# Row norms as a product with a diagonal matrix, in a two-block transformer kernel on one core

## The reference

```python
def rms_norm(x, g):
    xf = x.astype(jnp.float32)
    y = xf * lax.rsqrt(jnp.mean(xf * xf, axis=-1, keepdims=True) + EPS)
    return (y * g.astype(jnp.float32)).astype(x.dtype)

# first block, per layer: feed-forward, attention (forgetting or dilated), feed-forward
h = modulate(rms_norm(x, norm_g[i, 0]), shift[:, 0], scale[:, 0])
x = x + MACARON_WEIGHT * gate[:, 0, None, :] * swiglu(h, ...)

# second block, per layer: a mixer, then a convolutional feed-forward
h = rms_norm_2(x, norm_mix_pre[l]);  y = mixer(h);               x = x + rms_norm_2(y, norm_mix_post[l])
h = rms_norm_2(x, norm_ffn_pre[l]);  y = conv_ffn(h, ...);       x = x + rms_norm_2(y, norm_ffn_post[l])
```

## Time and profile before

| | |
|---|---|
| three timed runs | 1896.79, 1892.59, 1892.78 us; median 1892.78 |
| profiled execution | 1897.27 us, its span 1895.5 us, mean granted clock 0.98 |
| TensorE busy | 1805.1 us, 95% of the span |
| VectorE busy | 1463.1 us, 77% |
| ScalarE busy | 1053.0 us, 56% |
| chain that ended last | PE 75%, DVE 13%, issue 6%, ACT 4% |

### The profile page before, as it was taken

How to read it: one execution, slowest core, us unless ns; L and a number is a source line. 1 busy time by engine, 2 the same in 40 slices (tenths; PEclk the granted TensorE clock), 3 DMA queues, 4 the chain that set the end, 5 groups by cost and what they waited for, 6 DMA issues and landing times.

```text
span 1895.5 us, 28442 instructions
## 1 busy us (share of the span) xinstructions
PE 1805.1 (95%) x9778; PEld 1510.0 (80%) x9778; DVE 1463.1 (77%) x2268; ACT 1053.0 (56%) x1602; POOL 131.7 (7%) x170
## 2 busy tenths in 40 slices
PE   5999899899999999999999999999889998989998
PEld 4888677788878888788878888878678887768886
DVE  6888787688888887867755566557779966868994
ACT  5554465655445543655454455544776646666663
POOL 1101011000110110000000000000012200002210
PEclk9999999999999999999999999999999999889999
DMA  9878666377888786554530355554255454224553
GB/s 384 337 274 311 236 241 209 136 250 280 280 291 295 281 283 224 186 180 176 187 122 1 127 204 183 193 205 154 75 181 196 180 189 153 103 89 173 183 193 117
DMA packets 63778, 382.03 MB, mean 202 GB/s; under 512 B 7154, under 2 KB 7410, under 8 KB 27587
## 3 DMA queue, kind: packets, MB, share of 16 engines
q1 hardware_dynamic: 42912, 300.96, 44.3%
q0 software_dynamic: 20208, 78.79, 11.6%
q10 hardware_dynamic: 578, 1.22, 0.2%
HBM read 379.90 MB, written 1.05 MB: 201 GB/s over the span
## 4 chain that ended last, share of the span: by engine, by line
PE 75%; DVE 13%; issue 6%; ACT 4%; DMA 1%; DVEq 1%; SPq 0%; ACTq 0%
PE ps L560 18%; PE ps L477 11%; PE ps L479 10%; PE ps L478 10%; PE ps L562 9%; DVE ring_lo L1615 3%; DVE wb L1914 2%; PE ps L608 1%; PE ps L581 1%; PE ps L583 1%; PE ps L582 1%; PE ps L836 1%; PE ps L862 1%; DVE wa L1903 1%; PE ps L849 1%
## 5 line engine op out<-in xcount | busy, mean ns | idle before, releaser
L1615 DVE TENSOR_TENSOR ring_lo<-ring,w_hi 128x1024 fp32r<-128x1024 f32 x534 | 666.5, 1265 | 256.0 <-ACT w_hi L1130 254.5
L1130 ACT ACTIVATE w_hi<-ring 128x1024 fp32r<-128x1024 f32 x556 | 579.2, 1057 | 451.7 <-PE ps L479 269.3
L560 PE MATMUL ps<-h_both,w_hi 128*128 128x512 f32 x1984 | 700.8, 398 | 0.0
L562 PE MATMUL ps<-h_both,ring_lo 128*128 128x256 f32 x1984 | 557.6, 281 | 0.0
L560 PEld LDWEIGHTS ps<-h_both,w_hi 128*128 128x128 f32 x1984 | 373.4, 188 | 91.0
L562 PEld LDWEIGHTS ps<-h_both,ring_lo 128*128 128x128 f32 x1984 | 375.7, 189 | 0.0
L477 PE MATMUL ps<-w_hi,h_both 128*128 128x512 f32 x580 | 236.2, 407 | 7.6 <-DVE h_both L2348 3.4
L479 PE MATMUL ps<-w_hi,h_both 128*128 128x512 f32 x580 | 229.4, 395 | 0.0
L478 PE MATMUL ps<-ring_lo,h_both 128*128 128x512 f32 x580 | 228.9, 395 | 0.0
L477 PE MATMUL ps<-w_hi,hid_lo 128*128 128x512 f32 x456 | 180.3, 395 | 1.2 <-DVE ring_lo L1615 1.1
L479 PE MATMUL ps<-w_hi,hid_hi 128*128 128x512 f32 x456 | 177.6, 389 | 0.0
(11 more groups left out here) (360 smaller groups left out, 2150.9 us busy)
## 6 DMA issues: line engine op xcount, KB each, us to landing
ring<-in_stream SPq DMA_DIRECT2D x276, 1024.0 KB, 4.8
arena<-in_mod POOLq DMA_DIRECT2D x128, 512.0 KB, 5.7
arena<-in_mod SPq DMA_DIRECT2D x14, 512.0 KB, 13.9
gate<-in_wide POOLq DMA_DIRECT2D x3, 1536.0 KB, 10.0
arena<-in_nsaw POOLq DMA_DIRECT2D x2, 1072.0 KB, 9.0
ring<-in_stream SPq DMA_DIRECT2D x4, 512.0 KB, 15.1
arena<-in_konst POOLq DMA_DIRECT2D x1, 1295.5 KB, 8.7
arena<-in_mixw POOLq DMA_DIRECT2D x2, 576.0 KB, 10.5
```

The lines of the kernel that those rows point to most:

```text
L560: nc.tensor.matmul(ps[:, banks[b], :].rearrange("p (w t) -> p w t", w=2), hi, h_both[:, :, 2 * r + i, :], start=(r == 0 and i == 0), stop= ...
L562: mm = nc.tensor.matmul(ps[:, banks[b], T:2 * T], lo, h_hi[:, 2 * r + i, :], start=False, stop=(r == 3 and i == 1))
L1130: nc.scalar.activation(w_hi[:, q % SPLITS, :], ring[:, half % SLOTS, (q % 2) * QUARTER:(q % 2 + 1) * QUARTER], ACT.Copy).then_inc(w_hi_rea ...
L1615: v.tensor_tensor(ring_lo[:, slot, cs], ring[:, slot, cs], w_hi[:, q % SPLITS, :], ALU.subtract).then_inc(w_lo_ready, 1)
```

## The change

Norms 1 to 9 no longer form the scaled rows. A 128x128 diagonal matrix with the reciprocal roots of a tile's 128 tokens is formed (`rdiag`, 2 x 128 columns at the start of `xn`), and TensorE multiplies: chunk of x, stationary, by the diagonal. The result is the transposed and scaled chunk, as before. Norm 0 keeps its transposes.

- Tile 0's diagonal is formed by ScalarE (identity times the reciprocal), between the two halves of tile 1's squares. VectorE's reciprocal for it stands inside the update of x, between its last product and its last addition (`first_tile`).
- Tile 1's diagonal is formed by VectorE in `norm`, one instruction of 128 columns.
- In `update_normed` the first half of tile 1 is multiplied by the gate before the reciprocal is known (behind a new semaphore, `yms_half`), then scaled and added to x in one instruction.

```diff
+        rdiag = xn[:, 0, 0:2 * P]
...
@@ TensorE
-                        mm = turn(c, tt)
+            def norm(m):
+                for tt in range(NT):
+                    pe.wait_ge(xn_ready, 4 + 2 * (m - 1) + tt + 1)
+                    for c in range(KC):
+                        if c == 4 and tt == 0:
+                            pe.wait_ge(x_ready, 2 * m)
+                        b, o = norm_at(m, c)
+                        mm = nc.tensor.matmul(ps[:, b, o + tt * P:o + (tt + 1) * P], x[:, tt, c * P:(c + 1) * P], rdiag[:, tt * P:(tt + 1) * P], start=True, stop=True)
...
@@ ScalarE, norm
                 tick.mark(nc.scalar.activation(ms[:, 4:5], ms[:, 1:2], ACT.Identity, bias=eps_col))
+                act.wait_ge(rstd_ready, NT + m)
+                nc.scalar.activation(rdiag[:, 0:P], ident, ACT.Copy, scale=rstd[:, 0:1]).then_inc(xn_ready, 1)
                 act.wait_ge(x_ready, 2 * m)
...
@@ ScalarE, post_norm
-                tick.mark(nc.scalar.activation(ms[:, 6:7], ms[:, 3:4], ACT.Identity, bias=eps_col))
+                nc.scalar.activation(ms[:, 6:7], ms[:, 3:4], ACT.Identity, bias=eps_col).then_inc(yms_half, 1)
...
@@ VectorE
+            def first_tile(m):
+                dve.wait_ge(ms_ready, 2 * m + 1)
+                v.reciprocal(rstd[:, 0:1], rms[:, 0:1]).then_inc(rstd_ready, 1)
             def norm(m):
-                for tt in range(NT):
-                    dve.wait_ge(ms_ready, 2 * m + tt + 1)
-                    tick.mark(v.reciprocal(rstd[:, tt:tt + 1], rms[:, tt:tt + 1]))
-                    tick.settle()
-                    for half in (slice(0, 512), slice(512, D)):
-                        v.tensor_scalar(xn[:, tt, half], x[:, tt, half], rstd[:, tt:tt + 1], None, ALU.mult).then_inc(xn_ready, 1)
+                dve.wait_ge(ms_ready, 2 * m + 2)
+                tick.mark(v.reciprocal(rstd[:, 1:2], rms[:, 1:2]))
+                tick.settle()
+                v.tensor_scalar(rdiag[:, P:2 * P], ident, rstd[:, 1:2], None, ALU.mult).then_inc(xn_ready, 1)
...
@@ VectorE, update
+                    if lo == 512:
+                        first_tile(u + 1)
...
@@ VectorE, update_normed, tile 1
+                dve.wait_ge(yms_half, k + 1)
+                tick.mark(v.tensor_tensor(wb[:, 0:512], psf[:, o:o + 512], gate[:, s, 0:512], ALU.mult))
+                dve.wait_ge(yms_ready, 2 * k + 2)
+                tick.mark(v.reciprocal(rstd[:, 3:4], rms[:, 3:4]))
+                tick.settle()
+                v.scalar_tensor_tensor(out=x[:, 1, 0:512], in0=wb[:, 0:512], scalar=rstd[:, 3:4], in1=x[:, 1, 0:512], op0=ALU.mult, op1=ALU.add).then_inc(x_half, 1)
+                tick.mark(v.scalar_tensor_tensor(out=wb[:, 512:D], in0=psf[:, o + 512:o + D], scalar=rstd[:, 3:4], in1=gate[:, s, 512:D], op0=ALU.mult, op1=ALU.mult))
+                if k < 3:
+                    first_tile(7 + k)
+                tick.settle()
+                v.tensor_tensor(x[:, 1, 512:D], x[:, 1, 512:D], wb[:, 512:D], ALU.add).then_inc(x_ready, 1)
```

More of the change, by code:

```diff
@@ L345, in build @@
         mu_sum, cd_ready, csq_ready, var_sum, cn_ready, conv_hi, conv_out = [sem(n) for n in ("mu_sum", "cd_ready", "csq_ready", "var_sum", "cn_ready", "conv_hi", "conv_out")]
-        yms_ready, zvar_ready, zstd_ready, cstd_ready = [sem(n) for n in ("yms_ready", "zvar_ready", "zstd_ready", "cstd_ready")]
+        yms_ready, yms_half, zvar_ready, zstd_ready, cstd_ready = [sem(n) for n in ("yms_ready", "yms_half", "zvar_ready", "zstd_ready", "cstd_ready")]
         stored = sem("stored")
@@ L603, in hid_parts, with first_norm @@
                 return hid_hi[:, o:o + P], hid_lo[:, o:o + P]
[L605 to L608, removed]
+            def first_norm():
                 for tt in range(NT):
@@ L611, in norm @@
                         if c % 4 == 0:
-                            pe.wait_ge(xn_ready, 4 * m + 2 * tt + c // 4 + 1)
-                        if c == 4 and tt == 0 and m > 0:
+                            pe.wait_ge(xn_ready, 2 * tt + c // 4 + 1)
+                        b, o = norm_at(0, c)
+                        mm = nc.tensor.transpose(ps[:, b, o + tt * P:o + (tt + 1) * P], xn[:, tt, c * P:(c + 1) * P], ident)
+                        if tt == 1:
+                            mm.then_inc(norm_T, 1)
+            def norm(m):
[3 more added lines that the diff above has]
+                        if c == 4 and tt == 0:
                             pe.wait_ge(x_ready, 2 * m)
-                        mm = turn(c, tt)
+                        b, o = norm_at(m, c)
+                        mm = nc.tensor.matmul(ps[:, b, o + tt * P:o + (tt + 1) * P], x[:, tt, c * P:(c + 1) * P], rdiag[:, tt * P:(tt + 1) * P], start=True, stop=True)
                         if tt == 1:
@@ L1096, in _ @@
             pe.wait_ge(konst0_in, 16)
-            norm(0)
+            first_norm()
             ffn(0, False, 0)
@@ L1798, in update_normed @@
             def update_normed(k, s, bank):
[L1800 to L1810, removed]
+                o = bank * 512
+                dve.wait_ge(yms_ready, 2 * k + 1)
+                tick.mark(v.reciprocal(rstd[:, 2:3], rms[:, 2:3]))
+                tick.settle()
+                tick.mark(v.scalar_tensor_tensor(out=wa[:, :], in0=psf[:, o:o + D], scalar=rstd[:, 2:3], in1=gate[:, s, :], op0=ALU.mult, op1=ALU.mult))
+                tick.settle()
+                v.tensor_tensor(x[:, 0, :], x[:, 0, :], wa[:, :], ALU.add).then_inc(x_ready, 1)
+                o += D
+                dve.wait_ge(yms_half, k + 1)
+                tick.mark(v.tensor_tensor(wb[:, 0:512], psf[:, o:o + 512], gate[:, s, 0:512], ALU.mult))
+                dve.wait_ge(yms_ready, 2 * k + 2)
+                tick.mark(v.reciprocal(rstd[:, 3:4], rms[:, 3:4]))
+                tick.settle()
+                v.scalar_tensor_tensor(out=x[:, 1, 0:512], in0=wb[:, 0:512], scalar=rstd[:, 3:4], in1=x[:, 1, 0:512], op0=ALU.mult, op1=ALU.add).then_inc(x_half, 1)
+                tick.mark(v.scalar_tensor_tensor(out=wb[:, 512:D], in0=psf[:, o + 512:o + D], scalar=rstd[:, 3:4], in1=gate[:, s, 512:D], op0=ALU.mult, op1=ALU.mult))
+                if k < 3:
+                    first_tile(7 + k)
+                tick.settle()
+                v.tensor_tensor(x[:, 1, 512:D], x[:, 1, 512:D], wb[:, 512:D], ALU.add).then_inc(x_ready, 1)
             def ffn(f):
```

25 lines of the change are left out of this document (10 added, 15 removed).

## The result

The changed kernel took 1898.22 us (median of 7 executions, 1896.16 to 1899.31), the kernel before 1893.4 (7 executions, 1891.8 to 1896.79): a ratio of 1.0027, with a 95% interval of 1.0014 to 1.0040. That is 4.8 us more. It lies within the 0.3% that counted as no change (the interval reaches past it) and within the range of the forecast, but the forecast of the sum was +1.3.

What follows compares the result with a forecast made beforehand. TensorE, busy 95% of the span, was taken to bound the kernel, with idle gaps and half clock at the norms. Terms -2.1 + 0.5 + 1.3 + 2.3 - 0.7 = +1.3 us on the median gave 1894, range 1886 to 1902.

Steps and rivals of the forecast that it cites:

- the likeliest case: Whole kernel: the prediction's own forecast, 1894 us within 1889 to 1899, chance 0.60.
- The start: Ahead of norms 1 to 9: TensorE starts earlier, 0.74 us in norm 4, 0.48 in norm 2, 1.05 in norms 7 to 9.
- The records: TensorE in each norm: 16 more records of 0.113 us, 1.8 us more at full clock.
- the last rival: Products in nine norms: each costs as four transposes, 3.6 us more per norm, 1926 us in all; chance 0.03.
- The sum in norms 1 and 3 to 6: These five norms: -2.1 us for norms 1, 3, 5 and 6, +0.5 for norm 4.
- -2.1 us for norms 1, 3, 5 and 6: Gaps shrink from 2.1 to 1.4 us, the clock stays up, and 3.4 us at half clock per norm go.
- the +0.5 of norm 4: Norm 4, full clock before and after: 32 records end at 764.16, against big matmuls from 763.63 now.
- Norm 2: Norm 2: 1.81 us of added records less a start 0.48 earlier, +1.3 us.
- Norms 7 to 9: Each norm: 1.81 us of added records less a start 1.05 earlier, time at half clock kept; together +2.3 us.
- The end: Program's end: one product of 0.75 us leaves the chain before the last addition, -0.7 us.
- The rival of the falling clock: Norms 1, 3, 5 and 6: clock still falls in the short gaps, +4.3 for -2.1, total 1900.5 us; chance 0.20.
- the better clock: Norms 2, 7 to 9 and mixers: shorter gaps bring less time at half clock, total 1885 us; chance 0.17.

Runs made afterwards that it cites:

- before: The kernel before, unchanged, as the prediction's profile shows it: profiled execution 1897.27 us at a mean clock of 0.980; timed median 1893.4 us.
- again: The kernel before, unchanged, timed against itself and profiled a second time (execution of 1889.08 us): 1891.98 us, ratio 1.0003.
- e1: The kernel before with only the changed kernel's update (`update_normed`, `yms_half`), norms as before: 1889.16 us, ratio 0.9992 to the kernel before.
- e9: The changed kernel with identity products (5, 15 or 14) filling TensorE's wait ahead of each of norms 1 to 9: 1886.48 us, ratio 0.9972 to the kernel before.
- e8: The kernel before with the new update and identity products (6, 16 or 15) filling the wait ahead of norms 1 to 9: 1885.84 us, ratio 0.9963.
- e2: The changed kernel with one transpose of an `xn` block in place of each diagonal product, the norm's scaling left out: 1887.94 us, ratio 0.9976 to the kernel before.
- e7: The changed kernel's early start and update without its products: tile 0 scaled early by ScalarE and VectorE, all blocks transposed: 1888.35 us, ratio 0.9989 to the kernel before.
- e3: The changed kernel with products for tile 0 only; tile 1 scaled on VectorE and transposed as before: 1893.08 us, ratio 1.0009 to the kernel before.
- e11: The changed kernel with identity products (15 and 14) filling the wait ahead of norms 2 and 7 to 9 alone: 1890.1 us, ratio 0.9994 to the kernel before.

## Why the prediction was right, and where it was not

The result fell in the likeliest case, 0.8 us below its upper end. The sum under that case was +1.3 us where 4.8 was measured, so the hit owes more to the width of the case than to the sum. Step by step:

- **The start.** Forecast: gaps of 1.4 and 3.7 us, norm 2 0.48 us earlier. Measured: 1.29 to 1.34, 3.80, and 0.51 (3.96 for 4.47). ScalarE's matrix took 0.39 us where 0.30 was taken; it began earlier than thought, which made up for it. Tile 1 did not wait, and its root did not come 0.16 us later but at the old distance from the last large product, 2.64 us in norm 4.
- **The records.** 32 per norm, 0.115 us apart for the 0.113 taken. The rule of the last rival, four transposes per product ("TensorE: Matmul & The Clock Gate", section "Terms", in the Trainium skill) is not what these traces show: it is two.
- **The sum in norms 1 and 3 to 6.** The clock stayed up at these norms, as forecast, and the first large product of norm 4 came 2.82 us after the place of the old first transpose (both counted from the last large product), for 2.88. Here the size was off, and this is the term that failed: -2.1 us for norms 1, 3, 5 and 6. Two things were wrong with it. First, norm 1 has no such credit: the fall moved into the attention, and B is 27.19 us for a mean of 26.25 in the three profiles of the old norms (`before`, `again`, e1), +0.9 where -0.5 was forecast. Second, the credit of norms 3, 5 and 6 was read from one execution. Against that one, `before`, it is -1.5, as forecast. But B of these norms lies above its full-clock value (16.71, 16.71, 24.81) by 2.0, 0.3 and 0.9 us in the three profiles, 1.1 in the mean, and against the mean the changed kernel gains 0.6, since in norm 6 the products cost 0.6 (25.39 for 24.81). In exchange the +0.5 of norm 4 does not exist: VectorE's weight parts take it back. Norms 1 and 3 to 6 together: B of the changed kernel is 113.3 us, the mean of the three is 113.0. Forecast -1.6, measured +0.3.
- **Norm 2.** Forecast +1.3, measured 21.23 against a mean of 19.67 in the three: +1.6. In `before` alone, on which the forecast rests, B is 20.08: +1.15.
- **Norms 7 to 9.** Forecast +2.3. Measured 81.3 against 78.9, the mean of `before` and `again`: +2.4. The price is right, but the reason given for it, 16 more records at full clock behind an unchanged time at half clock, is only part: at full clock the products cost 1.1 us in these norms (74.9 in e9, 73.8 in e8). The rest is half clock, and it costs the two kinds of norm differently. Norm 7 of e1 and of the changed kernel, 6 us each:

```profile
1384.80:1390.80 6.00, 5.54 (x29) 0.72 0.99 321
1386.40:1392.40 6.00, 5.71 (x35) 0.72 0.97 315
```

Both have (1 - 0.72) x 12 = 3.4 us at 1.2 GHz. B of e1 is 0.1 us above that of e8, whose norm 7 is at full clock (23.50 for 23.37); B of the changed kernel is 1.75 above that of e9 (25.25 for 23.50), half of the 3.4. The transposes had slack beside the copies of the chunks (the wait of 0.92 us in e8) and the products have none. Over all norms half clock costs the changed kernel 8.2 us (against e9), e1 1.7 (against e8), or 2.7 with norm 1 left out, where its fall stands at the norm.
- **The end.** Forecast -0.7, measured -0.74.

These make +3.6 us (0.3 + 1.6 + 2.4 - 0.7) where +1.3 was forecast and 4.8 (2.7 to 7.6 by the interval) was measured; 1.2 us aren't located, and lie inside that interval.

The rival of the falling clock did not happen at the norms; in norm 1 it came true 14.6 us behind the last large product. That of the better clock did in part: over the products of norm 7 a reading of 0.69 is (1 - 0.69) x 2 x 5.09 = 3.2 us at half clock, where the earlier trace rows gives 4.9 over 6 us. No gain followed: the products pay for half of the time at half clock, as norm 7 shows above.

## What to carry to other kernels

Where TensorE stands idle ahead of short work on the way to a large stage, count that work at half clock and keep its records few; harmless products in the idle stretch can be worth more than an earlier start, if they end before it does. Follow a shift past the first instruction that it delays: half a microsecond at the first large product was worth nothing in norms 3 to 5, as the next wait was shorter by the same amount. Look at the next long wait, too, before you book a fall that is gone: in norm 1 it came back there. And set a clock credit read from one profile against a second profile of the same kernel before it enters a sum.

## What the runs showed of the hardware

**Loops at two rates.** In the looped products behind norms 7 and 9 (pairs of 512 and 256 columns) TensorE ran at one of two rates at a granted clock of 1.00, and the rate changed from execution to execution. The kernel before, `again` and the changed kernel, 50 us of each of the two loops:

```profile
1410.00:1460.00 50.00, 50.00 (x285) 1.00 0.52 187
1740.00:1790.00 50.00, 50.00 (x291) 1.00 0.53 189
```

```profile
1410.00:1460.00 50.00, 50.00 (x290) 1.00 0.53 191
1740.00:1790.00 50.00, 50.00 (x290) 1.00 0.53 189
```

```profile
1410.00:1460.00 50.00, 50.00 (x285) 1.00 0.52 189
1740.00:1790.00 50.00, 50.00 (x285) 1.00 0.52 187
```

A pair takes 0.353 us in the slower rate and 0.347 in the faster, which makes 2.2 us per loop (from the first large product of norm 9 to the end: 192.1 us in e8, 189.9 in e9). Of 14 profiles the slower rate stands in 5 behind norm 7 and in 6 behind norm 9, in kernels with and without products. The changed kernel's profile has it twice, that of before once. No run tells what chooses it, nor whether the change has a part in it.

**An fp32 product of 128 columns** is two records, a transpose one, each some 0.11 us behind the one before (32 records in 3.84 us in the changed kernel, 8 in 1.09 in e2). **ScalarE's copy of 128x128 with a scale per partition** took 0.39 us, VectorE's 0.29, where their plain copies take 0.29 and 0.23. **The clock** fell behind waits of 2.1 us in 9 of 12 cases (norms 1, 3, 5 and 6 in three profiles of the old norms) and never in norm 4; behind waits of 1.6 us in two of five (e7); behind 1.3 us in none of 15 in the changed kernel, e3 and e11, but in one of five in e2, where a second wait of 0.7 us follows; nor behind the 0.2 to 0.9 us that the filling left in e8 and e9.
